# Another order of the hybrid layer's small steps between the weight halves of its input projection

## The reference, cut to what matters

```python
z, xbc, dt_raw, q, k, v, f_raw = split(h @ w_in)             # 1024,1536,16,1024,1024,1024,8 columns
xbc = silu(causal_conv(xbc, conv_w, conv_b))                 # 4 taps, 1536 channels
xs, bm, cm = split(xbc)                                      # 16 heads of 64, 2 groups, state 128
y = ssd_chunked(xs, softplus(dt_raw + dt_bias), -exp(a_log), bm, cm)   # 2 chunks of 128 tokens
y = (y + d_skip * xs) * silu(z);  y_ssm = rms_norm per group of 512
o = softmax(q k^T / sqrt(128) + cumulated log-forget, causal) v        # 8 heads of 128
out = concat[y_ssm, o] @ w_out
```

## Time and profile before

| | |
|---|---|
| three timed executions | 2073.52, 2073.79, 2079.76 us; median 2073.79 |
| the profiled execution | span 2072.0 us from first to last instruction; the page gives no time beyond the span |
| busy | TensorE 2045.0 us (99%), VectorE 1432.5, ScalarE 1183.2, GpSimd 65.9 |
| mean granted TensorE clock | 0.998 |
| weights and other DMA | 372.56 MB, 180 GB/s |
| hybrid layer, z blocks and tail | about 1248.8 to 1426 us of the span |

### The profile page before, as it was taken

How to read it: one execution, slowest core, us unless ns; L and a number is a source line. 1 busy time by engine, 2 the same in 40 slices (tenths; PEclk the granted TensorE clock), 3 DMA queues, 4 the chain that set the end, 5 groups by cost and what they waited for, 6 DMA issues and landing times.

```text
span 2072.0 us, 27212 instructions
## 1 busy us (share of the span) xinstructions
PE 2045.0 (99%) x10690; PEld 1722.7 (83%) x10690; DVE 1432.5 (69%) x2056; ACT 1183.2 (57%) x1906; POOL 65.9 (3%) x101
## 2 busy tenths in 40 slices
PE   9999999999999999999999999999999999999998
PEld 6877888888887788888888878878888888887887
DVE  6987756774688875676576557776764776587763
ACT  5557566553546656655465457755553655486552
POOL 0001100000000300000000000000000000010000
PEclk9999999999999999999999999999999999999999
DMA  7572344555555244455455555515555555545553
GB/s 251 198 248 102 142 169 153 193 184 183 199 197 213 85 160 163 158 188 185 181 211 185 190 206 183 214 72 193 183 188 198 193 183 191 205 148 188 186 200 123
DMA packets 54902, 372.56 MB, mean 180 GB/s; under 512 B 7471, under 2 KB 7767, under 8 KB 11128
## 3 DMA queue, kind: packets, MB, share of 16 engines
q1 hardware_dynamic: 49392, 356.54, 47.9%
q10 hardware_dynamic: 4872, 12.70, 2.0%
q0 software_dynamic: 512, 1.57, 0.3%
HBM read 369.46 MB, written 1.34 MB: 179 GB/s over the span
## 4 chain that ended last, share of the span: by engine, by line
PE 92%; ACT 3%; DVE 3%; DMA 1%; issue 1%; POOL 0%; SPq 0%; DVEq 0%; POOLq 0%; ACTq 0%
PE ps L565 21%; PE ps L517 17%; PE ps L521 17%; PE ps L518 17%; PE ps L571 11%; PE ps L707 1%; DMA ring<-in_w 1%; PE ps L600 1%; PE ps L640 1%; PE ps L656 1%; PE ps L691 1%; ACT S L2390 1%; DVE ring_lo L1384 0%; PE ps L858 0%; PE ps L1205 0%
## 5 line engine op out<-in xcount | busy, mean ns | idle before, releaser
L1384 DVE TENSOR_TENSOR ring_lo<-ring,upper_w 128x1024 fp32r<-128x1024 f32 x435 | 526.2, 1224 | 201.6 <-ACT upper_w L2252 200.3
L2252 ACT CAST upper_w<-ring 128x1024 fp32r<-128x1024 f32 x435 | 450.4, 1052 | 276.1 <-DMA ring<-in_w 165.1
L518 PE MATMUL ps<-ring_lo,nT_pair 128*128 128x512 f32 x984 | 382.0, 388 | 0.0
L517 PE MATMUL ps<-upper_w,nT_pair 128*128 128x512 f32 x848 | 336.8, 397 | 2.8 <-DVE ring_lo L1384 2.1
L521 PE MATMUL ps<-upper_w,nT_pair 128*128 128x512 f32 x680 | 265.3, 390 | 0.0
L571 PEld LDWEIGHTS ps<-nT_pair,ring_lo 128*128 128x128 f32 x1920 | 246.2, 191 | 9.4
L571 PE MATMUL ps<-nT_pair,ring_lo 128*128 128x256 f32 x1920 | 249.0, 283 | 0.0
L518 PE MATMUL ps<-ring_lo,z_hi 128*128 128x512 f32 x624 | 242.9, 389 | 0.0
L565 PE MATMUL ps<-nT_pair,upper_w 128*128 128x512 f32 x960 | 230.0, 391 | 0.0
L518 PEld LDWEIGHTS ps<-ring_lo,nT_pair 128*128 128x128 f32 x984 | 185.0, 188 | 35.6
L565 PEld LDWEIGHTS ps<-nT_pair,upper_w 128*128 128x128 f32 x960 | 176.5, 188 | 34.3
(11 more groups left out here) (389 smaller groups left out, 2880.2 us busy)
## 6 DMA issues: line engine op xcount, KB each, us to landing
ring<-in_w SPq DMA_DIRECT2D x338, 1024.0 KB, 4.8
big<-in_gains ACTq DMA_DIRECT2D x7, 512.0 KB, 4.2
z<-in_mem ACTq DMA_DIRECT2D x2, 1024.0 KB, 7.8
big<-skew POOLq DMA_DIRECT2D x8, 192.0 KB, 6.8
x<-in_x SPq DMA_DIRECT2D x2, 512.0 KB, 7.3
ring<-in_w SPq DMA_DIRECT2D x2, 512.0 KB, 6.9
PTs<-skew ACTq DMA_DIRECT2D x1, 1024.0 KB, 4.5
big<-skew ACTq DMA_DIRECT2D x1, 1024.0 KB, 7.8
```

The source lines that it names most:

```text
L517: PE.matmul(out, hi, w_hi, start=start, stop=False)
L518: PE.matmul(out, hi, w_lo, start=False, stop=False)
L1384: V.tensor_tensor(ring_lo[:, q % RING, cols], ring[:, q % RING, cols], upper(n).bitcast(F32), ALU.subtract).then_inc(*lo_cut.up(h))
L2252: A.copy(upper(n), ring[:, q % RING, part * HALF:(part + 1) * HALF]).then_inc(*hi_cut.up(h))
```

## The change

The eight blocks are now computed in the order z0, z1, z2, z4, z3, z5, z6, z7 (queries and keys of the first heads, then those of the second), and the weight stream is in that order too. All small steps are placed by the count of halves over all eight blocks (0 to 31), through one `work` dictionary per engine. The convolution's tap instructions are done for two tiles per half, in the first six halves, in turn between the two tiles. The Silu of z is applied as z0 and z1 leave PSUM. The state matmuls come behind halves 17 to 19, scores and softmax of the attention from half 21 on, the y parts behind halves 25 and 26. The parts of y and of the heads change places in memory, the state's buffer and others too, the gain load moves into the layer, and fox units take the banks named below.

```diff
+Z_ORDER = (0, 1, 2, 4, 3, 5, 6, 7)
+Z_BANKS = {0: (0, 1), 1: (2, 3), 2: (0, 1), 4: (2, 3), 3: (0, 1), 5: (2, 3), 6: (0, 1), 7: (6, 7)}
+FOX_SCORES, FOX_TURNS, FOX_REAR = (4, 4, 4, 4), (6, 6, 0, 4), (2, 3, 1, 5)
...
-    QT, KTs = [ostage[...], tT[:, 8:12, :]], [acc[:, 0:4, :], nT[:, 4:8, :]]
+    QT, KT_ = ostage[:, :, :].rearrange("p t (a n) -> p (t a) n", a=2), acc[:, 0:4, :]
-    key_rows = [R[0][1], nT[:, 0:4, :]]
+    key_rows = R[1]
...
# TensorE: small steps behind half n
-            work = {0: sums, 2: lambda: to_rows(0), 5: lambda: to_rows(1), 7: products, 12: lambda: queries(0), 13: lambda: keys(0)}
-            work[15] = lambda: front(0)
...
+            work = {0: inputs, 2: sums, 7: lambda: to_rows(0), 8: lambda: to_rows(1), 9: products, 13: lambda: queries(0, (6, 7)),
+                    17: lambda: (keys(0, (6, 7)), within(1)), 18: lambda: (within(0), state()), 19: from_state,
+                    21: lambda: front(0), 22: lambda: (front(1), queries(1, (0, 1))), 23: lambda: middle(0), 24: lambda: middle(1),
+                    25: lambda: (keys(1, (2, 3)), y_parts(0, 2)), 26: lambda: (front(2), y_parts(4, 6)), 28: lambda: (back(0), front(3)),
+                    29: lambda: (back(1), middle(2)), 31: lambda: middle(3)}
+            for j, b in enumerate(Z_ORDER):
+                gemm(f"hyb.z{b}", lhs, Z_BANKS[b], beside=lambda c: work.get(4 * j + c, lambda: None)())
+                held(act_out.at(f"hyb.z{b}"), *Z_BANKS[b])
+            free(0, 2)
+            out_halves(0, 1)
             back(2)
             out_halves(1, 2)
             back(3)
# VectorE
-        def conv_taps(name, c, src, w, out):
-            for k in range(1, 4):
-                if k > 1:
-                    own()
-                V.scalar_tensor_tensor(out[:, c, :], ...)
+            def convs(q):
+                for k in range(1, 4):
+                    for c in (2 * q, 2 * q + 1):
+                        V.wait_ge(*(act_out.at(f"hyb.conv{c}") if k == 1 else dve_out.at(f"hyb.conv{c}.{k - 1}")))
+                        V.scalar_tensor_tensor(xbcT[:, c, :], ...)
...
+            work = {0: lambda: convs(0), 1: lambda: convs(1), 2: lambda: convs(2), 3: lambda: convs(3), 4: lambda: (convs(4), sums()), 5: lambda: convs(5),
+                    9: lambda: (state_inputs(0), decays(1)), 10: lambda: state_inputs(1), 11: lambda: skipped(0), 12: lambda: decays(0), 13: lambda: weigh(1),
+                    14: lambda: added(0), 15: lambda: skipped(1), 16: to_end, 17: lambda: weigh(0), 18: lambda: within(1), 19: lambda: (within(0), first_tokens()),
+                    20: from_state, 21: lambda: second_tokens(), 22: lambda: (scored(0), scored(1)), 23: lambda: mean_square("hyb.y", 4, 512, 0),
+                    24: lambda: (y_parts(), own(), middle(0), middle(1)), 25: lambda: added(1, (0,)), 26: lambda: (y_lo(0, 2), added(1, (1,))),
+                    27: lambda: (scored(2), y_lo(4, 6)), 29: lambda: (scored(3), back(0)), 30: lambda: (back(1), own(), middle(2)), 31: lambda: None}
# ScalarE
+            def spread_keys(hg):
+                A.wait_ge(*(dve_out.at("fox1.sc") if hg else sums_stored.at("keys")))
+                A.dma_start(key_rows..., scratch(...)).then_inc(*keys_loaded.up(hg, 16))
+            def inputs_done():
+                A.wait_ge(*dve_out.at("hyb.conv11"))
+                spread_rows(1)
+                A.activation(xbcT, xbcT, ACT.Silu).then_inc(*act_out.up("hyb.silu"))
+            work = {0: lambda: taps(0), 1: lambda: taps(1), 2: lambda: taps(2), 3: lambda: (taps(3), sums()), 4: lambda: taps(4), 5: lambda: (taps(5), spread_keys(0)),
+                    6: inputs_done, 8: lambda: to_rows(0), 9: lambda: (to_rows(1), spread_rows(0)), 10: lambda: (products(), state_decay(), decays(1, 0, 4)),
+                    11: lambda: decays(1, 4, 10), 12: lambda: decays(1, 10, 16), 13: lambda: decays(0, 0, 5), 14: lambda: (turned("Q", 0, QT, 6), decays(0, 5, 8)),
+                    15: lambda: decays(0, 8, 14), 16: lambda: decays(0, 14, 16), 18: lambda: turned("K", 0, KT_, 6), 19: state, 20: gain_of_output,
+                    21: lambda: squared_rows(0), 22: lambda: (front(0), squared_rows(1)), 23: lambda: (front(1), turned("Q", 1, QT, 0), spread_keys(1)),
+                    24: lambda: (middle(0), y_parts()), 25: lambda: middle(1), 26: lambda: (turned("K", 1, KT_, 2), y_hi(0, 2)), 27: lambda: y_hi(4, 6),
+                    28: lambda: front(2), 30: lambda: (front(3), middle(2))}
+                scaled(f"hyb.z{b}", ..., func=ACT.Silu if b < 2 else ACT.Copy)
...
-        next_gain(2)
         hybrid()
```

More of the change, by code:

```diff
@@ L197, in weight_stream @@
             w.add("hyb.dt", [at + 6], halves=1)
-    for b in range(8):
+    for b in Z_ORDER:
         w.add(f"hyb.z{b}", [at + 7 + 2 * b, at + 8 + 2 * b])
@@ L668, in cols_of, with attention @@
             return lambda c, t: buf[:, t, at + c * P:at + (c + 1) * P]
-        def attention(units, scores, ready, values=(), first=None, beside={}, by_act=False, between=None, amid={}, rear_banks=(6, 7), behind={}, within={}, by_hand=False):
+        def attention(units, scores, ready, values=(), first=None, beside={}, by_act=False, between=None, amid={}, rear_banks=(6, 7), behind={}, within={}, by_hand=False, front_banks=(0, 2), turn_banks=(4,)):
             n_ = len(units)
             def front(i):
-                b = 2 * (i % 2)
+                b = front_banks[i % len(front_banks)]
                 free(b, b + 1)
@@ L1139, in inputs @@
                 turn("hyb.cin", cols_of(z, H_X), 12, [act_out.at("hyb.x2")], lambda c: act_out.at(f"hyb.cin.{c}"), banks=(6, 7, 4, 5))
[L1140 to L1143, removed]
             def sums():
@@ L1189, in scores, with back @@
                     keys_ = slice(0, u_["nk"] * P)
-                    m = PE.matmul(o[:, h, keys_], QT[u_["hg"]][:, h, TOK[u_["t"]]], KTs[u_["hg"]][:, h, keys_], start=True, stop=True)
+                    m = PE.matmul(o[:, h, keys_], QT[:, h, TOK[u_["t"]]], KT_[:, h, keys_], start=True, stop=True)
                 return m
-            front, middle, back = attention(fox_units(), scores, lambda i: [act_out.at(f"hyb.K{i // 2}.2"), act_out.at(f"hyb.Q{i // 2}.2")], by_act=True,
-                                            rear_banks=(0, 7, 6, 7), by_hand=True)
-            work[15] = lambda: front(0)
[L1195 to L1198, removed]
+            front, middle, weighted = attention(fox_units(), scores, lambda i: [act_out.at(f"hyb.K{i // 2}.2"), act_out.at(f"hyb.Q{i // 2}.2")], by_act=True,
+                                                rear_banks=FOX_REAR, by_hand=True, front_banks=FOX_SCORES, turn_banks=FOX_TURNS)
+            def back(i):
+                PE.wait_ge(*act_out.at(f"hyb.z{6 + i // 2}"))
+                weighted(i)
             def within(t):
@@ L1208, in within, with state, from_state @@
                     held(dve_out.at(f"hyb.y{t}{g}"), y_banks[t][g])
[L1210 to L1224, removed]
+            def state():
+                PE.wait_ge(*dve_out.at("hyb.Xd"))
+                PE.wait_ge(*act_out.at("hyb.rows02"))
+                free(2, 3)
+                for g in range(2):
+                    m = PE.matmul(ps[:, 2 + g, :], z[:, 0, H_X + D + g * P:H_X + D + (g + 1) * P], Xd[:, g * 512:(g + 1) * 512], start=True, stop=True)
+                m.then_inc(*psum_full.up("hyb.S0"))
+                held(act_out.at("hyb.S0"), 2, 3)
+            def from_state():
+                PE.wait_ge(*act_out.at("hyb.S0"))
+                free(4, 5)
+                for g in range(2):
+                    m = PE.matmul(ps[:, 4 + g, :], CT[:, g, P:2 * P], S0[:, g * 512:(g + 1) * 512], start=True, stop=True)
+                m.then_inc(*psum_full.up("hyb.yo"))
+                held(dve_out.at("hyb.yo"), 4, 5)
             def out_halves(first, last):
@@ L1529, in add_x, with attention @@
             V.tensor_tensor(block_of(x, hf), block_of(x, hf), o, ALU.add).then_inc(*dve_out.up(event))
-        def attention(units, out, first=None, beside={}, by_act=False, between=None, second=None, amid={}, rear_banks=(6, 7), by_hand=False):
+        def attention(units, out, first=None, beside={}, by_act=False, between=None, second=None, amid={}, rear_banks=(6, 7), by_hand=False, front_banks=(0, 2)):
             def front(i):
-                s, b, u_ = i % 2, 2 * (i % 2), units[i]
+                s, b, u_ = i % 2, front_banks[i % len(front_banks)], units[i]
                 keys = slice(0, u_["nk"] * P)
@@ L2054, in added @@
             def added(hg, tokens=range(TT)):
-                own()
                 V.wait_ge(*keys_loaded.at(hg))
                 for t in tokens:
-                    if t and not hg:
-                        own()
+                    own()
                     for h in range(4):
                         c = cumq[:, t, 4 * hg + h:4 * hg + h + 1]
```

(39 more changed lines are left out.)

159 lines of the change are left out of this document (52 added, 107 removed).

## The result

The changed kernel took 2077.22 us (median of 20, 2076.09 to 2080.98) against 2073.28 (20 runs, 2071.21 to 2079.76): ratio 1.0019, 95% interval 1.0013 to 1.0025, that is 2.7 to 5.2 us slower. Predicted were 2076.5 and +2.7 against the first three runs; the forecast case came true. The slowdown is small, but its interval leaves out no change, where the prediction had held that less than 6.2 us can't be told.

What follows compares the result with a forecast made beforehand. TensorE, busy 2045.0 of 2072.0 us, was taken as the bound. New waits and clock, 5.2 + 1.8 + 1.5 + 0.4 + 1.2 = 10.1, less 7.2 removed, gave +2.9 and 2076.5 us against the median; range 2068.5 to 2081.

Steps and rivals of the forecast that it cites:

- the forecast case: Whole kernel slower by the new waits less the old tail, between 2073 and 2079.5 us; chance 0.50.
- The tail: After the eighth z block: TensorE's five waits, half clock and hidden idle time go, at most 7.2 us won.
- hidden tails: At each TensorE gap, idle time not shown because its start is modelled: 0.17 us each, 0.8 for five.
- places 8 to 22: Work behind weight halves 8 to 22 (row spreads, decays, state matmuls): inputs in time, 0 us of wait.
- The taps: Convolution, places 0 to 7: VectorE's cut and six taps outlast TensorE's half, so row transposes wait 5.2 us.
- The clock: After the wait at the row transposes: half clock costs TensorE 1.8 us, bounded by 0 and 3.6.
- z6 and z7: Waits for PSUM banks around the last two z blocks: 1.5 and 0.4 us near z6, 1.2 before z7.
- the turn of fox1: At place 24, transposing fox1's probabilities waits 0.4 us for banks 6 and 7, which ScalarE empties late.
- The sum: Whole kernel: 10.1 us of new waits and clock less 7.2 removed, +2.9 us.
- (a): Convolution in time, no early wait or half clock: -4.1 us, or -7.2 without the later waits; chance 0.24.
- (c): Early wait as forecast, but clock stays up and both bank waits vanish: 5.2 - 7.2, 2071.8 us; chance 0.12.
- Rival (b): Convolution taps gain nothing by interleaving, 0.52 us apart, wait 8.8 us: +6.5 to +8.3 us; chance 0.14.

Runs made afterwards that it cites:

- e10: Changed kernel with row transposes of xBC two halves later, their copies ahead of the decay exponentials, plus the edits of e3, e7 and e4: 2067.56 us, 0.9975.
- e7: Changed kernel with the second queries' copies ahead of fox1's exponentials and fox1's turned probabilities in banks 4 and 5, not 6 and 7: 2075.99 us, 1.0013.
- e3: Changed kernel with one swap on ScalarE, copies of the second queries ahead of fox1's exponentials: 2077.45 us, 1.0018.
- e9: Changed kernel as it is, traced and timed a second time: 2076.64 us, 1.0017 to the kernel before.
- e1: Changed kernel with each tile's three convolution taps done one after the other instead of in turn between two tiles: 2080.47 us, 1.0036.
- e5: Changed kernel with the row transposes of xBC behind halves 9 and 10 instead of 7 and 8, dependent small steps moved too: 2075.94 us, 1.0016.
- e4: Changed kernel with one swap on VectorE, lower parts of y groups 4 and 6 ahead of fox2's scale-and-add and maximum: 2076.05 us, 1.0014.
- e12: Changed kernel with the Silu of xBC in two pieces and the row spread issued behind it: 2074.11 us, 1.0008.
- e2: Changed kernel without the convolution's fourth tap, 12 of 36 tap instructions left out: 2071.50 us, 0.9994.

## Why the prediction was right

- **The tail.** "At most 7.2 us can be won": the five waits and the half clock there are gone, none is late next. e10 supports the amount: its distance of 131.96, less 0.8 of waits and two hidden tails of 0.17, is 130.8 for the bare work, and before stands 7.2 above that. For places 8 to 22 the forecast was 0, and no wait is found there.
- **The taps.** Forecast 3.53 us per place, 5.2 of wait. A place took 1.13 + 2.38 = 3.51 and the wait was 5.06. The whole chain ran 1.6 us later, as the layer began later, so the last tap ended at 1279.2 and not 1277.7.
- **The clock.** Taken 1.8, found 1.6 and 2.1 in two traces of the same kernel, and up to 2.9 (e7) after the same wait. The range of 0 to 3.6 held; the term is not fixed by the wait's length, so that 1.8 came this close is in part luck.
- **z6 and z7.** Forecast 1.5 + 0.4 and 1.2, found 1.7 + 0 and 1.4. The 0.4 was mis-sized: it needs TensorE to come to the turn of fox1 earlier, as it did in e3. So the walk was right about the queue, and wrong about which of two waits in a row is paid.
- **The sum.** +2.9, found +2.9 in the first pair of traces and +3.5 with e9. That the first pair agrees to 0.1 us is luck in part: the prediction counted 0.8 us of hidden tails among what goes and none for the three new waits, which hide 0.5; its 0.4 for the turn of fox1 and 0.2 too much for the clock made up for it. The timed difference is 3.9 (2.7 to 5.2), which holds both distances; the trace of the kernel before is a single one, so its own clock term of 1.7 to 1.8 may vary as well.
- **Rivals (a) and (c)** fall with the wait of 5.06 us, the half clock behind it and the two waits at banks.
- **Rival (b)** is shown false as a description of the changed kernel, and true as a mechanism: e1 is that kernel, at 1.0036. The Trainium skill (VectorE: DVE Perf Modes, "The DRAIN you can't avoid") says that the next operation does not start until the pipe is empty, and for a chain of copies that "the semaphore costs nothing extra here". The first does not hold for the taps in turn, which start 0.40 us apart at a length of 0.48; the section itself adds that an operation that is not held starts earlier, which the prediction left out. For the taps a semaphore on the neighbour is not free: six took 2.95 us dependent and 2.46 in turn.
- **What e5 taught.** My expectation for it took the walk of one engine (TensorE) and not ScalarE's queue behind the moved step. The prediction had done that walk; the experiment at first had not.

## What to carry to other kernels

When a step is pulled forward on the bound engine, sum the producers' work per slot before it: here VectorE had 3.5 us for each 2.7 us of TensorE, and six such slots put it 4.7 us behind, of a wait of 5.1. Where an engine's queue is in program order, a wait removed by a swap can show up at the next thing that the queue empties (a PSUM bank in e3; in e4 nothing came); walk the queue to its next consumer before taking the gain. Judge such edits by the distance between two marks with equal work between them, and take the cost of the clock out of it first: whole runs of one kernel scatter by 5 us and more, distances of one kernel by 0.6, and nearly all of that is clock.

## What the runs showed of the hardware beyond what was expected

After the same wait of 5.06 us the granted clock fell to the lower of its two levels (1.2 GHz) at different times: around the wait's end in one trace of the changed kernel (0.54 in the 3 us from 1282, 0.89 in the next three), from within the wait in the other (0.58 from 1277, 0.56 from 1282). The cost to TensorE was 1.6 to 2.9 us in five traces with this wait. Behind a wait of 3.0 us (e12) it was 1.7. In e2 a wait of 1.0 us was followed by no such stretch, as were all waits of up to 1.8 us before z6 and z7; the 1.9 us of the kernel before, with four shorter waits ahead of it, were followed by one. A tap instruction on 128x256 elements lasts 0.48 us. Two neighbouring ones start 0.40 us apart when independent, and 0.52 when the second needs the first: the chain of e1 then shows 0.49 to 0.50 and a gap of 0.02 to 0.03 as issue.
